# A decoder layer with a routed MoE: the overflow block moved directly behind the expert's gate-up

## The chip, the cores and the metric

The kernel runs on one core of a Trainium2 chip. The metric is the device time of one launch in microseconds, lower is better. All data is float32; TensorE (PE) multiplies, VectorE (DVE) and ScalarE (ACT) work on its results, GpSimd (POOL) does almost nothing here, and SyncE (SP) issues the DMAs that bring the weights from HBM.

## The reference

One layer of a decoder for 256 tokens of width 1024: a mixer of three kinds of attention, a layer norm, then a mixture of experts, and a second layer norm. Only the mixture of experts matters here. Each token goes to 4 of 32 experts, and each expert has 8 MB of gate-up weights (1024 x 2048) and 4 MB of down weights (1024 x 1024):

```python
logits = (xt @ router_w + router_b).astype(F32)
top_logit, top_e = lax.top_k(logits, TOP_K)            # 4 of 32
top_w = jax.nn.softmax(top_logit, axis=-1)
...
def expert_block(args):                                # for each expert's tokens
    e, tok, w = args
    xb = xt[tok]
    gu = xb @ w_gu[e] + b_gu[e]
    gate = jnp.minimum(gu[:, :D_EXPERT], SWIGLU_LIMIT)
    up = jnp.clip(gu[:, D_EXPERT:], -SWIGLU_LIMIT, SWIGLU_LIMIT)
    act = gate * jax.nn.sigmoid(SWIGLU_ALPHA * gate) * (up + 1.0)
    y = act @ w_dn[e] + b_dn[e]
    return (y * w[:, None]).astype(h.dtype)
...
out = jnp.zeros((T, D), h.dtype).at[buf_tok].add(ys.reshape(P, D))
```

All 402.7 MB of expert weights are read once.

## The kernel before

Every engine has its own program, written out by hand, and they are tied together by semaphores. After attention and routing (the first 200 us) the experts run in order 0 to 31, in a loop over 15 pairs (L1255 on PE) with the first and the last expert written out around it.

**Slots and overflow.** An expert has 64 slots (SLOTS). If more than 64 tokens chose it, the rest go in *extra blocks* of 32 slots (XSLOTS). How many extra blocks an expert has is known only at run time: a small table `nx` holds the counts, every engine reads its expert's entry into a register (`value_load`) and jumps over the extra block if it is zero.

**One expert on PE.** `gate_up` (L1109) multiplies the gathered tokens by the gate-up weights in four chunks of 2 MB, waiting for the DMA of each, and adds the bias with four short matmuls; each chunk counts up `guc`. DVE and ACT turn the result into activations (`activations`, L1687: minimum L1690, clip L1691, L1693, the sigmoid L714 on ACT, product L1696). Meanwhile PE fills the time: in an odd expert with `gather` (L1065), which gathers the tokens of the next pair of experts in two halves, copied out by ACT (L678); in an even expert with `combine` (L1073), which adds the outputs of a finished pair to the result in PSUM. Then `act_transposes` (L1144, its transposes are L1148) turns the activations, ACT copies them (L718), and `down` (L1133) multiplies by the down weights in four chunks of 1 MB, each counting up `dn_used`.

**One extra block on PE** (`extra_blocks`, L1214): it waits until two PSUM banks are free; gathers 32 tokens (`extra_gather`); ACT copies them (L691), two transposes (L1191), ACT copies again (L693); 36 gate-up matmuls, where each chunk counts up `xguc`; then it waits for activations of its own (DVE, ACT), transposes them (L1200, L1203), multiplies by the down weights (each chunk counts up `xdnc`), waits for ACT's copy of the result (L710) and adds it with `extra_combine`. DVE has its extra block behind the main activations, and prepares it ahead in `first_extra_slots` (L1740).

**The weights on SP.** There are two slots for gate-up weights, one for even and one for odd experts, and one slot for down weights. `next_gu` (L407) issues the gate-up weights of expert e+2 chunk by chunk (L354), as soon as expert e is through with that chunk; `next_dn` (L415) issues the down weights of e+1 (L359) as expert e is through with its own. SP runs them in one fixed order, gu of e+2, then dn of e+1, so that what stands behind waits for what stands in front (the last three pairs have the two the other way round). An expert with extra blocks is through with a chunk only when the block is, too:

```python
sp.wait_ge(s["guc"], i * (2 * GU_CHUNKS) + (par * GU_CHUNKS + c + 1))
sp.wait_ge(s["xguc"], xc)
load_gu(i + 1, par, c)
```

Line numbers of matmuls are those of the helper that issues them (L791 `mm`; transposes have the line of their call).

Of the kernel before, what the change touches and what calls it, by code (L numbers as in the profile page):

```python
# [57 lines left out]
def hybrid_layer(nc, x, w_in, b_in, pos_k, pos_v, w1_k, w2_k, w1_v, w2_v, g_out, w_out, ln1_g, ln1_b,  # L58
                 router_w, router_b, w_gu, b_gu, w_dn, b_dn, ln2_g, ln2_b, out):
    with ExitStack() as ctx:  # L60
# [480 lines left out]
        def _(act):  # L541
# [134 lines left out]
            def slots_to_sbuf(h, bank, n):  # L676
                act.wait_ge(s["ga"], n)
                act.activation(xg[:, 4 * h:4 * h + 4, :].rearrange("p k s -> p (k s)"), PB[bank][:, :], ACT.Copy)\  # L678
                   .then_inc(s["xg_ok"], 1)
# [6 lines left out]
            def extra_slots():  # L686

                act.reg_add(xcount, xcount, 1)
                xc = act.snap(xcount, min_val=1, max_val=96)
                act.wait_ge(s["xga"], xc)  # L690
                act.activation(xrows, PB[4][:, 0:256], ACT.Copy).then_inc(s["xgs"], 1)  # L691
                act.wait_ge(s["xgt"], xc)
                act.activation(yx[:, 0:KT * XSLOTS], PB[4][:, 256:512], ACT.Copy).then_inc(s["xxg"], 1)  # L693

            def extra_sigmoid():
                act.wait_ge(s["xgok"], act.snap(xcount, min_val=1, max_val=96))
                act.activation(act_x[0:64, :], gt[0:64, :], ACT.Sigmoid, scale=SWIGLU_ALPHA).then_inc(s["xsig"], 1)

            def extra_act_copy():
                xc = act.snap(xcount, min_val=1, max_val=96)  # L700
                act.wait_ge(s["xct"], xc)
                act.activation(CTx[:, :, :].rearrange("p b t -> p (b t)"), PB[7][:, 0:256], ACT.Copy)\
                   .then_inc(s["xctd"], 1)
                act.wait_ge(s["xat"], xc)
                act.activation(actTx[:, :, :].rearrange("p c s -> p (c s)"), PB[6][:, 0:256], ACT.Copy)\
                   .then_inc(s["xactT"], 1)

            def extra_outputs():
                act.wait_ge(s["xdnc"], act.snap(act.snap(xcount, min_val=0, max_val=96) * 4 + DN_CHUNKS, min_val=1, max_val=4 * 97))
                act.activation(yx, PB[6][:, :], ACT.Copy).then_inc(s["xyd"], 1)  # L710

            def sigmoid(n):
                act.wait_ge(s["g_ok"], n)
                act.activation(act_sb, gt, ACT.Sigmoid, scale=SWIGLU_ALPHA).then_inc(s["sig"], 1)  # L714

            def act_columns(bank, n):
                act.wait_ge(s["at"], n)
                act.activation(actT[:, :, :].rearrange("p c s -> p (c s)"), PB[bank][:, :], ACT.Copy)\  # L718
                   .then_inc(s["actT"], 1)

            def combine_weights(n):

                act.wait_ge(s["ct"], n)
                act.wait_ge(s["comb"], n)
                act.activation(CT[:, :, :].rearrange("p b t -> p (b t)"), PB[6][:, 0:256], ACT.Copy)\
                   .then_inc(s["ct_sb"], 1)

            def expert_output(e, n):
                act.wait_ge(s["dn_used"], n * DN_CHUNKS)
                act.activation(ysb[64 * e:64 * e + 64, 1, :], PB[7][64:128, :], ACT.Copy).then_inc(s["ysb_ok"], 1)  # L730

            def extra_blocks(t):
                n = act.value_load(nx[0:1, t:t + 1] if isinstance(t, int) else nx[0:1, bass.ds(t, 1)], min_val=0,
                                   max_val=MAX_EXTRA)
                with act.If(n > 0):
                    with act.Fori(0, n):
                        extra_slots()
                        extra_sigmoid()
                        extra_act_copy()
                        extra_outputs()  # L740
                act.nop()
# [10 lines left out]
            expert_output(0, 1)  # L752
            with act.Fori(0, PAIRS - 1) as i:
                sigmoid(2 * i + 2)
                slots_to_sbuf(0, 6, 2 * i + 3)
                act_columns(5, 2 * i + 2)
                slots_to_sbuf(1, 4, 2 * i + 4)
                extra_blocks(2 * i + 1)
                expert_output(1, 2 * i + 2)
                sigmoid(2 * i + 3)  # L760
                act_columns(5, 2 * i + 3)
                combine_weights(i + 2)
                extra_blocks(2 * i + 2)
                expert_output(0, 2 * i + 3)

            for b in range(TB):
# [16 lines left out]
        def _(pe):  # L783
# [6 lines left out]
            def mm(o, l, r, start, stop):  # L790
                return mm_(o, l, r, start=start, stop=stop, skip_group_check=True)  # L791
# [273 lines left out]
            def gather(h, bank, parts=range(4)):  # L1065
                for k in parts:
                    for b in range(TB):
                        ins = mm(PB[bank][:, P * k:P * k + P], x_sb[:, b, P * (4 * h + k):P * (4 * h + k) + P],
                                 oh[:, b, :], k == 0 and b == 0, b == TB - 1)
                if k == 3:  # L1070
                    ins.then_inc(s["ga"], 1)
# [8 lines left out]
            def gate_up_chunk(c, e):  # L1080

                for k in range(2 * c, 2 * c + 2):
                    for n in range(4):
                        ins = mm(PB[4 + n // 2][64 * (n % 2):64 * (n % 2) + 64, :], xg[:, k, 64 * e:64 * e + 64],
                                 gu_slot[e][:, k, 512 * n:512 * n + 512], k == 0, False)
                return ins
# [22 lines left out]
            def gate_up(e, loaded, n):  # L1109

                for c in range(GU_CHUNKS):
                    pe.wait_ge(s_gul[e][c], 16 * loaded)
                    gate_up_chunk(c, e).then_inc(s["guc"], 1)
                pe.wait_ge(s["oht"], n)
                gate_up_bias(e).then_inc(s["gu"], 1)
# [98 lines left out]
            def extra_blocks(e, loaded, t, pb4_pb6_copied, copies, outputs_copied):  # L1214

                count = pe.value_load(nx[0:1, t:t + 1] if isinstance(t, int) else nx[0:1, bass.ds(t, 1)], min_val=0,
                                      max_val=MAX_EXTRA)
                with pe.If(count > 0):
                    with pe.Fori(0, count):
                        pe.wait_ge(s[pb4_pb6_copied], copies)  # L1220
                        extra_gather()
                        for c in range(GU_CHUNKS):
                            extra_gate_up_chunk(c, e).then_inc(s["xguc"], 1)
                        extra_gate_up_bias(e).then_inc(s["xgu"], 1)

                        pe.wait_ge(s["ysb_ok"], outputs_copied + 1)
                        if not (isinstance(outputs_copied, int) and outputs_copied == 0):
                            pe.wait_ge(s["ysb_dv"], outputs_copied)
                        extra_act_transposes()
                        xc = pe.snap(xcount, min_val=1, max_val=96)  # L1230
                        pe.wait_ge(s["xctd"], xc)
                        pe.wait_ge(s["xactT"], xc)
                        for c in range(DN_CHUNKS):
                            pe.wait_ge(s_dnl[e][c], 16 * loaded)
                            extra_down_chunk(c).then_inc(s["xdnc"], 1)
                        extra_combine()
                pe.nop()
# [17 lines left out]
            with pe.Fori(0, PAIRS - 1) as i:  # L1255

                gate_up(1, i + 1, 2 * i + 2)
                pe.wait_ge(s["ohs"], i + 2)
                pe.wait_ge(s["ct_sb"], i + 1)
                gather(0, 6)  # L1260
                pe.wait_ge(s["g_ok"], 2 * i + 2)
                gather(1, 4, range(2))
                act_transposes(2 * i + 2)
                gather(1, 4, range(2, 4))
                extra_blocks(1, i + 1, 2 * i + 1, "xg_ok", 2 * i + 4, 2 * i + 1)
                down(1, i + 1, 2 * i + 2)

                pe.wait_ge(s["xg_ok"], 2 * i + 4)
                gate_up(0, i + 2, 2 * i + 3)
                pe.wait_ge(s["ysb_ok"], 2 * i + 3)  # L1270
                pe.wait_ge(s["ysb_dv"], 2 * i + 2)
                combine(range(3))
                act_transposes(2 * i + 3)
                weight_transposes()
                combine(range(3, 4))
                extra_blocks(0, i + 2, 2 * i + 2, "ct_sb", i + 2, 2 * i + 2)
                down(0, i + 2, 2 * i + 3)

            def outputs_of_30(b):
# [569 lines left out]
```

## Time and profile before

| what | value |
|---|---|
| median of 3 runs | 1151.54 us (1148.82 to 1151.68) |
| the profiled execution's own time | 1150.07 us |
| its span, on which all rows below stand | 1147.9 us |
| PE busy | 1073.4 us (94%) |
| DVE, ACT, POOL busy | 265.1, 152.4, 28.3 us |
| DMA moved | 426.32 MB, mean 371 GB/s |
| chain that ended last | PE 62%, DMA 30%, DVE 5% |

Times are microseconds from the start of the span. The time of the execution has 2.2 us around the span. "Busy" of PE counts pipelined matmuls with modelled ends, so 94% is not PE at its peak. The granted clock (PEclk) of 1.00 is 2.4 GHz, 0.50 is 1.2 GHz.

### The profile page before, as it was taken

To read this page: it belongs to the slowest core of one execution; us is meant where nothing else is said; L and a number is where in the kernel's file an instruction comes from. 1 tells how busy PE (TensorE), PEld (TensorE's weight loads), DVE (VectorE), ACT (ScalarE), POOL (GpSimd) and SP (SyncE) were. 2 spreads that over 40 slices of the span, in tenths; PEclk is the share of its full clock that TensorE was granted. 3 is DMA by queue.
4 is the path that set the end of the run, shared out by engine and by line. 5 is a ranking of instruction groups with operands and counts; after the bars stand their busy time and mean duration, and the time that the engine had idled before them with its cause. 6 is when DMAs were issued, how large, how long until landed. Compare 5 with 4: busy or idle time off the path is not lost.

```text
span 1147.9 us, 14752 instructions
## 1 busy us (share of the span) xinstructions
PE 1073.4 (94%) x5382; PEld 463.7 (40%) x5383; DVE 265.1 (23%) x770; ACT 152.4 (13%) x318; POOL 28.3 (2%) x54
## 2 busy tenths in 40 slices
PE   7999897998999999999999979999999999999995
PEld 6777644332343443323333333434343324343332
DVE  2354636111112111111111211121111111111124
ACT  2044511110010110100000010101010101010120
POOL 3000410000000000000000000000000000000000
PEclk9999998999999999999999989999999999999998
DMA  9723439939999999999999999999999999999993
GB/s 309 263 110 74 148 132 395 400 149 399 423 426 425 427 427 426 427 427 425 427 427 425 429 417 399 427 427 426 427 427 426 427 421 426 427 425 427 427 425 157
DMA packets 49268, 426.32 MB, mean 371 GB/s; under 512 B 5065, under 2 KB 8954, under 8 KB 16442
## 3 DMA queue, kind: packets, MB, share of 16 engines
q1 hardware_dynamic: 48666, 425.37, 89.7%
q10 hardware_dynamic: 576, 0.61, 0.2%
q8 instruction: 16, 0.26, 0.1%
q14 instruction: 10, 0.08, 0.0%
HBM read 424.91 MB, written 1.05 MB: 371 GB/s over the span
## 4 chain that ended last, share of the span: by engine, by line
PE 62%; DMA 30%; DVE 5%; issue 1%; SPq 1%; ACT 1%; DVEq 0%
PE PB L791 59%; DMA WB<-in_w_down_dram 26%; DMA WB<-in_w_gate_up_dram 3%; PE PB L1148 1%; DMA WB<-in_w_in_dram 1%; DVE S L1693 1%; DVE S L1696 1%; DVE S L1690 1%; DVE S L1691 1%; DVE S L1555 0%; DVE S L1815 0%; SPq L337 0%; DVE WB L1474 0%; DVE S L1589 0%; DVE K L1806 0%
## 5 line engine op out<-in xcount | busy, mean ns | idle before, releaser
L791 PE MATMUL PB<-WB,S 128*64 128x512 f32 (+5 forms) x3456 | 753.2, 590 | 31.1 <-DMA WB<-in_w_down_dram 24.2
L791 PEld LDWEIGHTS PB<-WB,S 128*64 128x64 f32 (+2 forms) x3456 | 253.5, 139 | 509.5 <-issue 441.7
L1690 DVE TENSOR_SCALAR S<-PB 128x512 f32<-128x512 f32 (+1 forms) x34 | 23.5, 691 | 482.1 <-PE PB L791 482.1
L791 PE MATMUL PB<-S 32*64 32x512 f32 (+5 forms) x464 | 108.7, 586 | 4.7 <-issue 2.4
L1734 DVE COPY S<-PB 64x512 f32<-64x512 f32 x31 | 21.2, 683 | 264.6 <-PE PB L791 264.6
L714 ACT ACTIVATE S<-S 128x512 f32<-128x512 f32 x32 | 20.2, 632 | 456.2 <-DVE S L1690 456.1
L791 PEld LDWEIGHTS PB<-S,X 128*128 128x128 f32 x512 | 62.7, 200 | 13.3 <-issue 12.2
L791 PE MATMUL PB<-S,X 128*128 128x128 f32 x512 | 66.8, 286 | 1.0 <-DVE S L1633 1.0
L791 PE MATMUL PB<-S,WB 128*128 128x256 f32 (+2 forms) x336 | 60.2, 377 | 1.0 <-DMA WB<-in_w_in_dram 0.6
L791 PEld LDWEIGHTS PB<-S 32*64 32x64 f32 (+5 forms) x464 | 33.0, 147 | 67.6 <-issue 62.1
L791 PE MATMUL PB<-WB 128*32 128x128 f32 (+9 forms) x284 | 48.1, 362 | 5.3 <-DVE WB L1520 2.8
L791 PEld LDWEIGHTS PB<-S,WB 128*128 128x128 f32 (+1 forms) x336 | 46.5, 170 | 12.4 <-issue 2.1
L730 ACT ACTIVATE S<-PB 64x512 f32<-64x512 f32 x31 | 18.4, 595 | 240.7 <-PE PB L791 240.7
L791 PEld LDWEIGHTS PB<-WB 128*64 128x64 f32 (+3 forms) x284 | 30.3, 153 | 18.7 <-issue 12.6
L530 POOL TENSOR_TENSOR K<-K 128x1 f32<-128x1 f32 x4 | 3.1, 766 | 968.3 <-DVE K L1809 956.5
L718 ACT ACTIVATE S<-PB 128x512 f32<-128x512 f32 x32 | 19.1, 598 | 56.7 <-PE PB L1148 56.7
L1148 PEld LDWEIGHTS PB<-K,S 128*128 128x128 f32 x128 | 18.1, 210 | 17.2 <-DVE S L1696 16.4
L1148 PE MATMUL PB<-K,S 128*128 128x128 f32 x128 | 23.7, 308 | 1.4
L1696 DVE TENSOR_TENSOR S<-S 128x512 f32<-128x512 f32 (+1 forms) x34 | 23.5, 691 | 1.8 <-ACT S L714 0.7
L1693 DVE SCALAR_TENSOR_TENSOR S<-S 128x512 f32<-128x512 f32 (+1 forms) x34 | 23.5, 692 | 1.2
L1691 DVE TENSOR_SCALAR S<-PB 128x512 f32<-128x512 f32 (+1 forms) x34 | 23.2, 682 | 0.1
L678 ACT ACTIVATE S<-PB 128x512 f32<-128x512 f32 x32 | 19.1, 598 | 20.8 <-PE PB L791 20.8
(219 smaller groups left out, 353.1 us busy)
## 6 DMA issues: line engine op xcount, KB each, us to landing
WB<-in_w_gate_up_dram SPq DMA_DIRECT2D x128, 2048.0 KB, 24.8
WB<-in_w_down_dram SPq DMA_DIRECT2D x128, 1024.0 KB, 21.1
WB<-in_w_in_dram SPq DMA_DIRECT2D x3, 2048.0 KB, 16.0
WB<-in_w_in_dram SPq DMA_DIRECT2D x1, 2144.0 KB, 11.0
WB<-in_w_in_dram SPq DMA_DIRECT2D x2, 1024.0 KB, 10.8
WB<-in_w_out_dram SPq DMA_DIRECT2D x2, 1024.0 KB, 10.0
WB<-in_w_out_dram SPq DMA_DIRECT2D x1, 2048.0 KB, 7.9
WB<-in_w_in_dram SPq DMA_DIRECT2D x1, 1040.0 KB, 12.7
```

The source lines that it names most:

```text
L530: pool.tensor_tensor(st[:, o + 2:o + 3], st[:, o + 1:o + 2], half[:, 0:1], ALU.pow).then_inc(s["lnp"], 1)
L678: act.activation(xg[:, 4 * h:4 * h + 4, :].rearrange("p k s -> p (k s)"), PB[bank][:, :], ACT.Copy)\
L714: act.activation(act_sb, gt, ACT.Sigmoid, scale=SWIGLU_ALPHA).then_inc(s["sig"], 1)
L718: act.activation(actT[:, :, :].rearrange("p c s -> p (c s)"), PB[bank][:, :], ACT.Copy)\
L730: act.activation(ysb[64 * e:64 * e + 64, 1, :], PB[7][64:128, :], ACT.Copy).then_inc(s["ysb_ok"], 1)
L791: return mm_(o, l, r, start=start, stop=stop, skip_group_check=True)
L1148: ins = tr(PB[5][:, P * c:P * c + P], every_fourth(act_sb, c), ident)
L1690: ts(g, gate, LIMIT, None, ALU.min).then_inc(s[g_ok], 1)
L1691: ts(u, up, LIMIT, -LIMIT, ALU.min, ALU.max).then_inc(s[clip], 1)
L1693: stt(u, u, 1.0, g, ALU.add, ALU.mult).then_inc(s[upg], 1)
L1696: tt(a, u, a, ALU.mult).then_inc(s[done], 1)
L1734: cp(ysb[64 * e:64 * e + 64, 0, :], PB[7][0:64, :]).then_inc(s["ysb_dv"], 1)
```

## The change

In the loop over pairs the extra block moves. In the odd expert of a pair it stood behind `gather` and `act_transposes`, directly ahead of `down`; now it stands directly behind `gate_up`, ahead of `gather`. In the even expert it stood behind `combine` and the transposes; now it stands ahead of `combine`. What it waits for at its start is now `g_ok`, DVE's minimum, which frees the PSUM bank PB4 (it was ACT's copy of the gathered tokens in the odd, and of the combine weights in the even expert). ACT's program is put in the same order: its extra block follows the sigmoid. DVE, SP, the blocks of experts 0 and 31, and the work itself stay as they are.

```diff
@@ ACT, loop over pairs
                 sigmoid(2 * i + 2)
+                extra_blocks(2 * i + 1)
                 slots_to_sbuf(0, 6, 2 * i + 3)
                 act_columns(5, 2 * i + 2)
                 slots_to_sbuf(1, 4, 2 * i + 4)
-                extra_blocks(2 * i + 1)
                 expert_output(1, 2 * i + 2)
                 sigmoid(2 * i + 3)
+                extra_blocks(2 * i + 2)
                 act_columns(5, 2 * i + 3)
                 combine_weights(i + 2)
-                extra_blocks(2 * i + 2)
                 expert_output(0, 2 * i + 3)
@@ PE, loop over pairs
                 gate_up(1, i + 1, 2 * i + 2)
                 pe.wait_ge(s["ohs"], i + 2)
                 pe.wait_ge(s["ct_sb"], i + 1)
+                extra_blocks(1, i + 1, 2 * i + 1, "g_ok", 2 * i + 2, 2 * i + 1)
                 gather(0, 6)
                 pe.wait_ge(s["g_ok"], 2 * i + 2)
                 gather(1, 4, range(2))
                 act_transposes(2 * i + 2)
                 gather(1, 4, range(2, 4))
-                extra_blocks(1, i + 1, 2 * i + 1, "xg_ok", 2 * i + 4, 2 * i + 1)
                 down(1, i + 1, 2 * i + 2)
 
                 pe.wait_ge(s["xg_ok"], 2 * i + 4)
                 gate_up(0, i + 2, 2 * i + 3)
+                extra_blocks(0, i + 2, 2 * i + 2, "g_ok", 2 * i + 3, 2 * i + 2)
                 pe.wait_ge(s["ysb_ok"], 2 * i + 3)
                 pe.wait_ge(s["ysb_dv"], 2 * i + 2)
                 combine(range(3))
                 act_transposes(2 * i + 3)
                 weight_transposes()
                 combine(range(3, 4))
-                extra_blocks(0, i + 2, 2 * i + 2, "ct_sb", i + 2, 2 * i + 2)
                 down(0, i + 2, 2 * i + 3)
```

## Rows read from the trace of the kernel before

**Rows 1.** The page: what the DMA engines moved in 40 equal slices.

```profile
GB/s 309 263 110 74 148 132 395 400 149 399 423 426 425 427 427 426 427 427 425 427 427 425 429 417 399 427 427 426 427 427 426 427 421 426 427 425 427 427 425 157
```

**Rows 2.** The chain that ended last, in order of time: start, length, what.

```profile
296.63 25.50 PE PB L791 x130
...
349.37 25.50 PE PB L791 x130
...
467.00 27.29 DMA WB<-in_w_down_dram
...
496.53 27.27 DMA WB<-in_w_down_dram
...
1086.81 4.72 PE PB L791 x24
```

**Rows 3.** Timeline, the lines with LDWEIGHTS show the wait: PE at the extra block of expert 1.

```profile
241.45 1.09 PE L791 MATMUL PB<-S 32*64 32x512 f32 x8
...
242.61 0.69 DVE L1690 TENSOR_SCALAR S<-PB 128x512 f32<-128x512 f32 x1 [10.97 <-PE PB L791]
...
245.99 1.06 PE L791 MATMUL PB<-S,X 128*128 128x128 f32 x8
...
247.08 0.60 ACT L678 ACTIVATE S<-PB 128x512 f32<-128x512 f32 x1 [0.30 <-PE PB L791]
...
247.86 1.07 PE L791 MATMUL PB<-X,S 128*32 128x256 f32 x16 [0.82 <-ACT S L678]
...
250.34 7.07 PE L791 MATMUL PB<-WB,S 128*32 128x512 f32 x64 [0.47 <-ACT S L693]
...
263.05 5.28 PE L791 MATMUL PB<-WB,S 128*32 128x512 f32 x32 [0.52 <-issue]
...
270.96 20.82 PE L791 MATMUL PB<-WB,S 128*64 128x512 f32 x96
```

**Rows 4.** Timeline of SP: the issues behind the extra block of expert 1.

```profile
252.49 5.47 SPq L354 DMA_DIRECT2D WB<-in_w_gate_up_dram  x4
273.16 5.48 SPq L359 DMA_DIRECT2D WB<-in_w_down_dram  x4
```

**Rows 5.** The same behind the extra block of expert 15.

```profile
668.53 5.46 SPq L354 DMA_DIRECT2D WB<-in_w_gate_up_dram  x4
689.55 5.48 SPq L359 DMA_DIRECT2D WB<-in_w_down_dram  x4
```

**Rows 6.** Stretches: length, busy of PE, PEld, DVE, ACT, POOL; PEclk, DMA share, GB/s.

```profile
245.00:249.00 4.00, 3.12 (x32) 2.11 (x30) 0.67 (x3) 1.36 (x4) 0.00 (x0) 1.00 0.00 0
...
261.00:265.00 4.00, 3.00 (x18) 1.43 (x22) 0.42 (x1) 0.77 (x2) 0.00 (x0) 0.75 1.00 430
...
273.00:277.00 4.00, 4.00 (x20) 1.29 (x18) 0.00 (x0) 0.00 (x0) 0.00 (x0) 1.00 0.85 276
...
670.00:672.00 2.00, 2.00 (x25) 0.52 (x17) 0.00 (x0) 0.00 (x0) 0.00 (x0) 1.00 0.85 344
```

**Rows 7.** Timeline: PE behind the gate-up of expert 30.

```profile
1090.39 3.86 PE L791 MATMUL PB<-S 32*64 32x512 f32 x14
...
1094.34 0.75 PE L1148 MATMUL PB<-K,S 128*128 128x128 f32 x4
...
1096.10 10.52 PE L791 MATMUL PB<-WB,S 128*64 128x512 f32 x48
```

**Rows 8.** Timeline: PE around its first jump over an extra block (expert 0).

```profile
211.02 1.18 PEld L791 LDWEIGHTS PB<-S 128*128 128x128 bf16 x10
...
212.43 0.19 PEld L791 LDWEIGHTS PB<-S 128*128 128x128 f32 x1 [0.24 <-issue]
...
217.58 0.70 PE L791 MATMUL PB<-S 128*128 128x512 f32 x1 [2.41 <-issue]
```

**Rows 9.** Who waited for whom: total us, times, longest.

```profile
DVE K L1764 <- issue: 17.2, 16, 1.4
```

**Rows 10.** DMA queues, only 300 to 640 us: packets, MB, share.

```profile
q8 instruction: 1, 0.02, 0.0%
```

## The prediction

> **What bounds the kernel now.** I read the page's slices first. From the tenth slice to the last but one the DMA engines move 425 to 427 GB/s almost without a gap [rows 1]: the expert weights alone are 402.7 MB, 943 us at 427 GB/s. So the experts are bound by the stream of weights, and what can be won is the time in which the stream stands still. PE's 94% busy must not mislead; the chain shows who is late. An expert costs PE 26.4 us where the chain runs on PE alone (52.74 us from one x130 group to the next, which is a pair) and 29.5 us where it runs over the landing of down weights [rows 2]. PE has 3.1 us to spare for each expert and catches up after each delay. The stream is hurt only where SP has nothing to issue.
>
> Next, where the overflow blocks are. The narrow matmuls (128*32) occur in two places in the whole trace, at expert 1 (248 to 271 us) and, with the same pattern, at expert 15 (664 to 687 us). Both are odd. The other 28 experts in the loop jump over the block. Around expert 1 the stream stands completely still until gate-up weights are issued at 252.49 us, and after them it has a second, smaller hole: 276 instead of 427 GB/s around 273 us [rows 4, 6]. Around expert 15 there is hardly a first hole (344 GB/s for 2 us at 670 us) and then one at 690 us, with the down weights issued at 689.55 us [rows 5, 6].
>
> **What the change does to the two blocks.** The block moves ahead of the 16 gathering matmuls (of 128 columns) and the four transposes. Before: the bias of gate-up ends at 241.45 + 1.09 = 242.54 us, and the block's own gather begins at 247.86, 5.32 us later [rows 3]. Of these, 4.51 us are work (to 245.99 + 1.06 = 247.05), 0.81 is the wait for ACT's copy. After: the block waits for DVE's minimum, which ends at 242.61 + 0.69 = 243.30 us. Before, the block began 0.18 us behind the copy (247.08 + 0.60 = 247.68); with the same step it will begin at 243.48. It starts **4.4 us earlier**, and so does `xguc`: SP issues gate-up weights for expert 3 at about 248.1 us instead of 252.49, and those for expert 17 at about 664.1 instead of 668.53 [rows 4, 5].
>
> **Why this brings next to nothing.** SP has a fixed order: behind four chunks of gate-up weights come four of down weights, and these wait for `down` of the same expert. The four gate-up chunks are 8.39 MB, 19.6 us at 427 GB/s. Issued at 252.49 they keep the engines busy to about 273 us, and the down weights are issued at 273.16: the two just meet. Issued at 248.1 they are through at about 269, and **the stream stands still for the same 4.4 us behind them**, since `down` is still last on PE. Its start was the gate-up's end + 4.51 (gather, transposes) + 0.81 (wait) + 23.10 (the block, 247.86 to 270.96) = 28.42 us. It becomes 0.94 (wait for DVE) + 23.10 + 4.51 = 28.55. Sum: +0.13 us for a block. A few terms come off or on: the transposes waited 0.1 us or so for the main activations, which are now long done. ACT reads its count behind the sigmoid now (DVE's reading and jumps show 17.2 us in 16 cases, 1.1 each, 1.4 at most [rows 9]); that runs in the shadow of PE's gather in the block, and costs up to 0.7 us where it doesn't. I take +0.1 for a block, between -0.8 (the wait vanishes) and +0.8. For expert 15 the working is the same; the small hole at 670 us closes (344 of 427 GB/s for 2 us is 0.4 us) and opens again ahead of 690.
>
> What is queued behind the new waits: on PE everything, but it is the same work in another order, and none of the delayed pieces has a user before `down`: ACT's copies of the gathered tokens lie under `down`, 16 matmuls of two passes each, 32 of the 96 that take 20.82 us, so 6.9 us [rows 3]. The block now asks for expert 15's down weights 4.4 us earlier, near 675 instead of 679 us; the hole at 670 shows that SP's queue had run dry, so all that was issued before had arrived [rows 6]. On SP nothing is moved. DVE's order stays; its activations of the block still wait for the block's gate-up, 14 us behind the minimum.
>
> Do both additions reach the end? Yes: with the down weights' issue the stream starts again and doesn't stop, so 0.1 us there is 0.1 us at the end, twice: **+0.2 us**.
>
> **TensorE's clock** is the largest uncertain term. In both blocks PE waits some 3 us for the block's activations, and the granted clock is 0.75 in the mean of 261 to 265 us [rows 6], a mix of 2.4 and 1.2 GHz. The block's 32 rows of down matmuls take 5.28 us; its 64 rows of gate-up take 7.07, so 32 would take 3.54 at full clock [rows 3]. The low clock costs 1.74 us a block. The wait stays, so I leave the term as it is; but the stretch of low clock may come to lie wholly in the wait (-1.74), or reach further, over the gather that now follows (+1.74). Two blocks: -3.5 to +3.5 us, both ends unlikely.
>
> **What it does to the experts without a block.** PE reads the count and jumps directly behind the gate-up. For 27 of the 28 the price is under the 3.1 us that PE has to spare [rows 2]. Not so for expert 30, behind which nothing is left to catch up: its last gate-up chunk lands at 1086.8 us and from there the chain is PE's [rows 2]. There, bias and three combine matmuls end at 1090.39 + 3.86 = 1094.25, and the transposes, which wait for the activations, begin at 1094.34 [rows 7]. The cover is 0.09 us; whatever stands between bias and combine beyond that is on the path. How long does PE stand at a read and a jump? Before, at expert 0: eight short bf16 matmuls, the read, the jump, then combine, whose weight loads follow with the usual idle of 0.24 us and not more [rows 8]. So at most 0.24, and I take 0, since PE's front has 4.7 us of matmuls (last chunk and bias) in hand to run ahead, against 1.4 at most for DVE's read. In the old place, ahead of `down`, it was free as well: the 1.76 us from 1094.34 to 1096.10 are filled by six transposes (four take 0.75) and a combine matmul ((3.86 - 1.09) / 3 = 0.92) [rows 3, 7]. So nothing comes back.
>
> **Forecast: no difference that can be measured.** 1150.07 + 0.2 = 1150.3 us for the profiled execution. Against the median of the runs, 1.5 us above it, 1151.54 + 0.2 = **1151.7 us**.
>
> **Rivals.**
> First, **faster, since the stream starts earlier**. The gate-up slot is given back 4.4 us sooner; if the time behind it were not taken back by the down weights, the kernel would win 4.4 us at expert 1 and the 0.4 us of the hole at expert 15: 4.8 us, 1146.7 us. For it: the still stand before 252.49 us is the longest in the experts (0 GB/s from 245 to 249 us [rows 6]). Against it: down weights are issued at 273.16, exactly where the gate-up weights end, and 276 GB/s there shows that the engines have nothing else [rows 4, 6]. Its weaker form is a clock that falls better, up to -3.5. Chance 5% for over 0.3%.
>
> Second, **slower, by the jump behind the gate-up**. Place: expert 30, and the start of both blocks. Behind the very first jump over an extra block PE stood for 2.41 us with nothing to wait for ("issue") in the midst of a combine [rows 8]. If a jump in its new place brings such a stop each time, it costs 2.41 - 0.09 = 2.3 us at expert 30, and at the two blocks what a read (1.4 us) takes beyond the wait of 0.81, 0.6 each: 3.5 us, 1155.1 us. It decides from 0.09 us on at expert 30; at the others PE's 3.1 us cover it. Against it: from 300 to 640 us, some twelve experts with as many jumps, the queue of instruction fetches has a single packet [rows 10], so the loop's code isn't fetched anew, and I take the 2.41 us for those of a first passage. The Trainium skill (Runtime: NRT & Kernel Launch, Instruction fetch mechanics) has a rule that speaks for this rival: a taken branch out of the fetched window stalls the engine until the page is there. The trace doesn't bear it out for a repeated loop. Chance 7%, with a clock that falls worse 9% for all over 0.3%.
>
> Third, **the change reaches more experts than two**: that in even experts the block no longer waits for `combine_weights`. It can't, since no even expert has a block; the time is that of the forecast, and it is in its chance.
>
> **How the numbers follow.** Forecast 86%, first rival 5%, second with the clock 9%. A measurement of this kernel tells 0.3%, 3.45 us, from no change. The range takes in the terms of the sum (-0.8 to +0.8 a block, most of the clock's swing, up to 2.3 at expert 30), and leaves the first rival's full size out: 1148.3 to 1155.1 us.
>
> **What would show it.** In the profile of the changed kernel: the narrow gather begins 0.8 to 1.0 us behind the bias, at 243.5 us (step 1); SP's gate-up issue behind expert 1 is at 248.1 (step 2); the down weights' issue stays at 273.2 to 273.4 and 689.6 to 689.9, and the stream has a hole of over 4 us ahead of it (step 3); the transposes of expert 30 still begin 0.1 us behind the third combine (step 4). I am wrong if the down weights' issue comes over 1 us sooner or later, which would be the clock or PE's front, or if the stream has no hole there.

## The result: 2 us slower, within what counts as no change

| | before | changed |
|---|---|---|
| median (20 runs each) | 1150.47 us | 1152.49 us |
| lowest, highest | 1148.82, 1152.61 | 1149.42, 1154.98 |
| ratio, 95% interval | | 1.0017 (1.0009 to 1.0024) |
| profiled execution, its span | 1150.07, 1147.9 us | 1152.66, 1150.5 us |

The forecast was 1151.7 us and no measurable difference. The ratio is 2.0 us of loss (1.0 to 2.8), clear of zero and below 3.45 us. The forecast's +0.2 us is too small; where the rest comes from is what the experiments are about. That 1151.7 lies only 0.8 us from 1152.49 is in part luck: it was built on a median of three runs, 1151.54, which is 1.1 us above the median of twenty, and this offsets more than half of the 1.8 us that the forecast lacks.

First the page of the changed kernel, what the DMA engines moved in 40 slices. It answers to [rows 1]:

```profile
GB/s 311 269 101 74 158 131 394 406 196 334 425 427 424 427 426 427 427 426 427 426 427 426 427 416 369 426 427 426 427 425 426 427 423 426 427 426 427 426 426 159
```

The stream has the same two dips. In the first the ninth slice has 196 GB/s instead of 149, the tenth 334 instead of 399: the gate-up weights come earlier, and the standstill has moved behind them.

The timeline of PE and its neighbours in the changed kernel, at the block of expert 1, answers to [rows 3]:

```profile
240.72 1.09 PE L791 MATMUL PB<-S 32*64 32x512 f32 x8
241.87 0.69 DVE L1690 TENSOR_SCALAR S<-PB 128x512 f32<-128x512 f32 x1 [10.97 <-PE PB L791]
242.75 1.07 PE L791 MATMUL PB<-X,S 128*32 128x256 f32 x16 [0.94 <-DVE S L1690]
...
244.31 0.44 PE L1191 MATMUL PB<-K,S 128*128 128x128 f32 x2 [0.50 <-ACT S L691]
...
245.23 8.77 PE L791 MATMUL PB<-WB,S 128*32 128x512 f32 x64 [0.47 <-ACT S L693]
...
259.63 5.03 PE L791 MATMUL PB<-WB,S 128*32 128x512 f32 x32 [0.52 <-issue]
...
267.30 2.94 PE L791 MATMUL PB<-S,X 128*128 128x128 f32 x24
...
270.08 0.64 PE L1148 MATMUL PB<-K,S 128*128 128x128 f32 x4
...
271.54 20.82 PE L791 MATMUL PB<-WB,S 128*64 128x512 f32 x96
```

Everything before it ran 0.73 us earlier than in the profile of before, so stretches are to be compared, not points in time. The order is the new one: the narrow gather begins 0.94 us behind the bias (240.72 + 1.09 = 241.81), the wide gather stands behind the block. One length is not as before: the 64 rows of the block's gate-up take 8.77 us instead of 7.07.

SP's issues in the changed kernel, behind expert 1 and behind expert 15, answer to [rows 4, 5]:

```profile
248.93 5.60 SPq L354 DMA_DIRECT2D WB<-in_w_gate_up_dram  x4
273.74 5.48 SPq L359 DMA_DIRECT2D WB<-in_w_down_dram  x4
...
666.07 5.47 SPq L354 DMA_DIRECT2D WB<-in_w_gate_up_dram  x4
692.18 5.48 SPq L359 DMA_DIRECT2D WB<-in_w_down_dram  x4
```

And stretches of 2 us of the changed kernel (columns as in [rows 6]), first in the block's gate-up, then ahead of the issue of the down weights at 273.74:

```profile
244.00:246.00 2.00, 1.21 (x10) 0.43 (x14) 0.93 (x3) 0.64 (x2) 0.00 (x0) 0.86 0.00 0
246.00:248.00 2.00, 2.00 (x16) 0.58 (x12) 0.00 (x0) 0.00 (x0) 0.00 (x0) 0.50 0.00 0
248.00:250.00 2.00, 2.00 (x20) 0.52 (x16) 0.00 (x0) 0.00 (x0) 0.00 (x0) 0.79 0.26 49
...
268.00:270.00 2.00, 2.00 (x21) 2.00 (x20) 0.00 (x0) 0.60 (x1) 0.00 (x0) 1.00 0.93 393
270.00:272.00 2.00, 2.00 (x17) 1.62 (x17) 0.00 (x0) 0.95 (x2) 0.00 (x0) 1.00 0.04 8
272.00:274.00 2.00, 2.00 (x12) 0.72 (x10) 0.00 (x0) 0.25 (x1) 0.00 (x0) 1.00 0.00 0
```

The kernel before, in the last 2 us ahead of its issue of the down weights at 273.16:

```profile
271.00:273.00 2.00, 2.00 (x12) 0.73 (x12) 0.00 (x0) 0.00 (x0) 0.00 (x0) 1.00 1.01 434
```

Two things are seen. The granted clock is 0.50, that is 1.2 GHz, from 246 to 248 us, in the middle of dense matmuls; that is the longer gate-up. And the stream stands still for some 4 us ahead of the down weights (8 and 0 GB/s), where the kernel before has full speed, 434 GB/s, up to 273 us.

Where the 2.6 us between the two profiled spans lie:

| stretch | before | changed | difference |
|---|---|---|---|
| start to the bias of expert 1 | 241.45 | 240.72 | -0.73 |
| bias to the issue of down weights, expert 1 | 31.71 | 33.02 | +1.31 |
| from there to the bias of expert 15 | 384.35 | 384.31 | -0.04 |
| bias to the issue of down weights, expert 15 | 32.04 | 34.13 | +2.09 |
| from there to the end | 458.35 | 458.32 | -0.03 |

The first row lies ahead of all that was changed; it is what one execution differs from another. Of the rest every difference lies between gate-up and down weights of the two experts with a block. The 28 others, and the tail behind expert 30, give nothing.

### The profile page after: what moved, and what is told of

It is laid out like the page before. It is cut to its first block, busy times and chain, and to the rows that moved or that the text cites. A ratio compares the mean times of both kernels' runs of the same rounds, so it can differ in the third digit from the quotient of the medians.

```text
span 1150.5 us, 14750 instructions
## 1 busy us (share of the span) xinstructions
PE 1076.6 (94%) x5382; PEld 464.2 (40%) x5383; DVE 264.9 (23%) x770; ACT 151.9 (13%) x318; POOL 28.3 (2%) x54
## 4 chain that ended last, share of the span: by engine, by line
PE 62%; DMA 30%; DVE 5%; issue 1%; SPq 1%; ACT 1%; DVEq 0%
PE PB L791 59%; DMA WB<-in_w_down_dram 26%; DMA WB<-in_w_gate_up_dram 3%; PE PB L1148 1%; DMA WB<-in_w_in_dram 1%; DVE S L1690 1%; DVE S L1693 1%; DVE S L1696 1%; DVE S L1691 1%; DVE S L1555 0%; DVE S L1815 0%; SPq L337 0%; DVE WB L1474 0%; DVE S L1589 0%; DVE K L1806 0%
```

## The experiments

The theory: nothing is lost in the order as such; **the clock** is. In the new order a stretch of 1.2 GHz falls into the block's gate-up, where it hadn't been in the profile of before. Rivals: the luck of one profile (it falls where it will, in either order, and the 2 us come from elsewhere), and the jumps directly behind the gate-up. In the following, "path" is the stretch from the bias to the issue of down weights, first for expert 1, then for expert 15; "gate-up" and "down" are the times that the block's 64 gate-up and 32 down matmuls of the trace take, its rows.

### Both kernels again, and the two halves of the change

The changed kernel once more:

> The changed kernel, unaltered, a second profile and more times. Clock theory (the order brings a stretch of 1.2 GHz into the block's gate-up, since the pauses now lie directly behind the expert's gate-up): the 64 rows of the block's gate-up take 8.3 to 8.8 us in both blocks again, not the 7.07 of before, and the ratio is 1.001 to 1.0025. Rival, luck of one profile (the low stretch may fall anywhere in either order): at least one of the two takes 7.07 us here. Rival, the jumps in even experts: gate-up may take anything, the tail behind expert 30 is longer than before by 1 us or more.

Measured: 1.0012 (1.0003 to 1.0020). Gate-up 8.64 and 7.07 us, path 32.79 and 31.93. The transposes of expert 30 begin 0.09 us behind the third combine, as before. The ratio is as the theory said, but its "both blocks" is wrong, and the luck rival's condition is met by the second block.

The odd experts' half alone, as diff against before:

```diff
@@ PE
                 pe.wait_ge(s["ct_sb"], i + 1)
+                extra_blocks(1, i + 1, 2 * i + 1, "g_ok", 2 * i + 2, 2 * i + 1)
                 gather(0, 6)
...
                 gather(1, 4, range(2, 4))
-                extra_blocks(1, i + 1, 2 * i + 1, "xg_ok", 2 * i + 4, 2 * i + 1)
@@ ACT
                 sigmoid(2 * i + 2)
+                extra_blocks(2 * i + 1)
                 slots_to_sbuf(0, 6, 2 * i + 3)
                 act_columns(5, 2 * i + 2)
                 slots_to_sbuf(1, 4, 2 * i + 4)
-                extra_blocks(2 * i + 1)
```

> Only the odd experts' block is moved, the even experts' stays behind combine. Clock theory: both blocks that run are odd, so the whole loss is here, +1.9 us, ratio 1.001 to 1.0025, block gate-ups of 8.3 to 8.8 us. Jump rival: most of the loss is gone, ratio under 1.0007.

Measured: 1.0033 (1.0020 to 1.0046), gate-up 8.56 and 7.07, down 6.53 and 6.00, path 34.36 and 32.59. The whole loss is here, and more than was expected; five runs don't say whether it really is more than the full change's, whose interval it overlaps.

The even experts' half alone is the rest of the change's diff:

> Only the even experts' block is moved; none of them has one, so what is moved is the reading of the count and the jump, behind the gate-up. Clock theory: nothing, ratio 0.9993 to 1.0007, and the transposes of expert 30 begin 2.8 us behind the start of the minimum as before. Jump rival: +1.5 us or more, ratio 1.0013 or above, and a gap on TensorE between bias and combine.

Measured: 1.0005 (0.9995 to 1.0014), path 31.71 and 31.58. PE's timeline in the even half alone, behind the gate-up of expert 30:

```profile
1091.22 3.86 PE L791 MATMUL PB<-S 32*64 32x512 f32 x14
1095.17 0.74 PE L1148 MATMUL PB<-K,S 128*128 128x128 f32 x4
```

1091.22 + 3.86 = 1095.08, and 0.09 us later the transposes: the same as [rows 7], with the reading of the count and the jump now in between. The jump rival is out at expert 30, the place where nothing would have covered it. The interval alone would leave room for 1.6 us in all, but the odd half has the whole loss and none of these jumps in the even experts.

The kernel before once more:

> The kernel before, unaltered, for a second profile. Clock theory: the block's gate-up takes 7.07 us in both blocks, the block's down 5.3 us. Luck rival: one of the gate-ups takes over 8 us here.

```profile
247.88 8.77 PE L791 MATMUL PB<-WB,S 128*32 128x512 f32 x64 [0.47 <-ACT S L693]
...
665.75 7.07 PE L791 MATMUL PB<-WB,S 128*32 128x512 f32 x64 [0.47 <-ACT S L693]
```

That is the timeline of PE in this second profile of before. The theory's expectation is wrong: the low stretch falls into the gate-up in the old order, too, here at expert 1. So it can't be "the new order has it, the old one not". What is left is a matter of how often. This execution also shows one source of the swing from run to run (3.8 us over 20 runs of the kernel before, 5.6 of the changed one) that has nothing to do with the change: the bias of expert 1 comes at 238.99 instead of 241.45 us. From 216 to 224 us, behind the jump over expert 0's block, the granted clock is 1.00 in the mean here and 0.79 in the first profile, and the way from there to the bias of expert 1 is 1.3 us shorter.

### Filling the pauses

If the clock falls for the pauses ahead of the block's gate-up, matmuls in these pauses must keep it up. The fillers multiply the identity by a tile into PSUM bank PB7, and nobody reads the result. The block's two waits for the copies out of PB7 move to its start (this part of the edit is not shown):

```diff
+            def filler(columns, n=1):
+                for _ in range(n):
+                    mm(PB[7][:, 0:columns], ident, x_sb[:, 0, 0:columns], True, True)
 ...
+                        filler(512)
                         pe.wait_ge(s[pb4_pb6_copied], copies)
 ...
+                filler(256)
                 pe.wait_ge(s["xgs"], xc)
 ...
+                filler(256)
                 pe.wait_ge(s["xxg"], xc)
```

> The changed kernel with idle matmuls (identity by a tile, into a free PSUM bank, not used) in the three short pauses at the start of a block: 0.86 us in the wait for the minimum, 0.43 us in each of the two waits for ACT's copies. Clock theory (the low stretch in the block's gate-up follows from the pauses before it): both gate-ups take 7.07 us, ratio against before near 1.000 (0.999 to 1.001), some 1.9 us under the changed kernel. Chance rival (the low stretch falls where it will, whatever PE does before): one gate-up in two still takes over 8 us, ratio 1.001 to 1.002.

Measured: 1.0041 (1.0027 to 1.0054). Gate-up 7.07 and 7.07, as the clock theory said, and path 32.25 and 32.18 against the 33.02 and 34.13 of the changed kernel. But the time is worse, by 4.7 us against before, where at most some 1 us had been expected. The stretches say where: the bias of expert 1 comes at 243.34 us, later than in any profile so far (238.99 to 242.09). The loss is ahead of the first block.

> The changed kernel with three idle matmuls (2.6 us) in the block's wait for its activations alone. Clock theory: the block's down rows take 3.5 us instead of 4.9 to 6.4, in both blocks, 1.5 to 3 us less each; the gate-up keeps its lottery; ratio against before 0.998 to 0.9995. Chance rival: the down rows stay at 5 us or more, ratio 1.001 to 1.002.

Here three fillers of 512 columns stand in the wait for the block's activations, behind the bias of its gate-up. Measured: 1.0027 (1.0017 to 1.0037), slower than expected. Down rows 3.64 and 3.64 us, with a granted clock of 1.00 all through them; gate-up 8.53 and 8.77; path 31.49 and 31.73. And again a late start: bias at 244.82 us. PE's timeline of this kernel around its first jump, which answers to [rows 8]:

```profile
211.32 1.04 PE L791 MATMUL PB<-S 128*128 128x256 bf16 x8
217.01 3.57 PE L791 MATMUL PB<-S 128*128 128x512 f32 x4 [4.65 <-issue]
```

The stop behind the jump over expert 0's block is 4.65 us and comes ahead of the combine's float32 passes. In [rows 8] it was 2.41 us and stood ahead of the combine's last pass, and it is 1.5 to 2.4 us in all eleven profiles whose expert 0 has the block as it was. The stop does not end later, though: PE goes on 6.8 to 7.7 us behind the start of expert 0's bias in all fourteen profiles, the three with fillers there (6.9 to 7.3) among them. What differs is how much PE had done before it stood.

> The same three idle matmuls in the order of before. Clock theory: down rows at 3.5 us, 1.7 us less for each block, ratio 0.996 to 0.998 (-2.5 to -4.5 us). Chance rival: no change, 0.9995 to 1.0005.

The same in the old order. Measured: 0.9994 (0.9985 to 1.0003), down rows 3.64 and 3.64, gate-up 7.07 and 8.77, path 30.06 and 31.75, the stop 4.92 us. The mechanism is there, the gain is not: three fillers in a pause win some 1.6 us a block, and their code in expert 0's block costs 3 to 4 us once: from the bias of expert 0 to that of expert 1 it is 34.2 to 34.8 us in the three kernels with fillers there, and 29.5 to 31.6 in the eleven others.

So the fillers were put into the loop's odd block alone:

> The changed kernel with idle matmuls in the three pauses at the start of a block, as in fill_start, but only in the loop's odd block, so that the code of expert 0's block keeps its length. Clock theory: both gate-ups of the blocks take 7.07 us; from the bias of gate-up to the issue of down weights 32.2 us as in fill_start (32.25 and 32.18). Code-length theory of fill_start's loss (added code in expert 0's block lengthens the one stop behind the first jump from 1.9 to 4.6 us): the stop is 1.8 to 2.4 us here, ratio against before 1.000 to 1.0015, under fill_start by 2 to 4 us. Rival (the idle matmuls themselves cost): ratio 1.003 or more.

Measured: 1.0004 (0.9995 to 1.0013). Gate-up 7.07 and 7.07, path 32.43 and 32.35, the stop 1.52 us. By the ratios that is +0.5 us, 4.2 us less than fill_start, so the fillers themselves are not what cost there, and 1.5 us less than the changed kernel, whose interval this one overlaps. Its timeline and stretches at expert 1, to be read beside those of the changed kernel above:

```profile
243.24 1.12 PE L791 MATMUL PB<-X,K 128*128 128x512 f32 x2
244.30 1.07 PE L791 MATMUL PB<-X,S 128*32 128x256 f32 x16
245.30 0.70 PE L791 MATMUL PB<-X,K 128*128 128x256 f32 x2
245.87 0.44 PE L1197 MATMUL PB<-K,S 128*128 128x128 f32 x2
246.15 0.60 PE L791 MATMUL PB<-X,K 128*128 128x256 f32 x2
...
246.00:248.00 2.00, 1.96 (x16) 0.76 (x20) 0.44 (x3) 0.38 (x1) 0.00 (x0) 1.00 0.00 0
248.00:250.00 2.00, 2.00 (x24) 0.65 (x20) 0.00 (x0) 0.00 (x0) 0.00 (x0) 1.00 0.33 66
```

The three lines with "PB<-X,K" are the fillers; PE has no pause, and the clock stays at 1.00.

All profiles together, the gate-ups of the blocks that took 8.3 to 8.8 us instead of 7.07:

| order at the block (early pauses filled or not) | profiles | gate-ups with low clock |
|---|---|---|
| as before, pauses not filled | 6 | 2 of 12 |
| as changed, pauses not filled | 5 | 7 of 10 |
| as changed, pauses filled | 3 | 0 of 6 |

(The experiments on delays and fill_wait_before count in the first row, fill_wait and work_in_wait in the second, work_and_fill in the third; those on delays and on real work follow below.) If the order made no difference, 7 of 10 against 2 of 12 or more extreme would come in 1.7% of cases, and 7 of 10 against 0 of 6 in 1.0% (in this direction alone). The difference sits at expert 1 (5 of 5 against 1 of 6); at expert 15 it is 2 of 5 against 1 of 6, which shows nothing by itself. It is not proof of each block, but it is how the sum comes out: a low stretch costs 1.3 to 1.7 us, and half a one more for each block makes +1.6 us for the two. That is near the 2.0 measured.

The runs that were not profiled have a record, too: the mean granted clock of each. It is 0.982 or less in 14 of 32 runs of the changed kernel and in 2 of 68 runs of the kernel before, 0.9823 and 0.9841 in the mean. As an estimate, 0.0018 of 1150 us is some 2 us, which is what the difference costs if PE is busy all through it. And in the twenty runs of the table above, the ten with 0.982 or less took 1153.4 us in the mean, the ten others 1151.1. The record doesn't say where in a run the clock was low: fill_start_odd has 0.9826 in the mean of its 11 runs, as low as the changed kernel, and loses hardly anything. Its stretches at the blocks' wait and down rows have 0.74 in the mean over 13 us (254 to 267 and 671 to 684), the first profile of before has 0.87 and 0.74, the second 0.87 and 0.87; while PE waits, a low clock costs nothing.

### Does a microsecond at the block reach the end, and one elsewhere not?

Three fillers (2.6 us) ahead of `down`, in the order of before, once in the odd blocks (the first lines) and once in the 13 odd experts that have none (the last):

```diff
                         extra_combine()
+                        if delayed:
+                            filler(512, 3)
 ...
+                with pe.If(count < 1):
 ...
+                    filler(512, 3)
 ...
                 down(1, i + 1, 2 * i + 2)
```

The second also reads the count once more ahead of this, and waits for the copies out of PB7 ahead of the fillers.

> The order of before with three idle matmuls (2.6 us) at the end of each odd block, ahead of down. Theory (the issue of down weights behind a block restarts the stream, so each us there is a us at the end): two blocks, +5.1 us, ratio 1.0035 to 1.0055; clock may shift it by 1 us. Rival (the stream's start, set by the gate-up slots, is what counts): ratio 0.9995 to 1.001.

Measured: 1.0051 (1.0038 to 1.0064), +5.9 us, path 35.38 and 35.60 instead of some 31.9. What is lost between gate-up and down weights at a block is lost at the end.

> The order of before with the same 2.6 us of idle matmuls ahead of down in the 13 odd experts of the loop that have no block, 33 us in all. Theory (PE has 3.1 us to spare for each expert): +0 to +0.5 us, ratio 0.9995 to 1.001. Rival (PE is the bound): up to +33 us, ratio 1.01 to 1.03.

Measured: 1.0081 (1.0068 to 1.0094), +9.1 us of the 33 added. Neither answer. Its path and the 384 us between the blocks are untouched (31.65, 384.04, 32.16); all of it lies behind expert 15, 467.26 us instead of 458.35. The chain of waits of this kernel says why:

```profile
712.11 25.50 PE PB L791 x130
...
768.02 25.50 PE PB L791 x130
...
823.92 25.50 PE PB L791 x130
...
1047.48 25.50 PE PB L791 x130
```

55.9 us for each pair, and the chain is on PE and the activations to the end; before it was 52.7 us [rows 2], and the chain was back on the DMA by 853 us. As an estimate from these: PE recovers 6.3 us with each pair (59.0 - 52.7), and it took some three pairs, so after a block PE is some 20 us behind. With the delays it recovers only 3.1 us a pair and never gets the chain back to the DMA before the experts end. From 900 to 950 us the stream itself falls to 392 GB/s, where it had 426. PE's spare time is free only once it has caught up.

### Real work instead of idle matmuls

The wait of 3.1 us for the block's activations can take work that has to be done anyway: the main transposes and the half of the gather that goes to bank PB4. `extra_body` is the block of `extra_blocks` with these two behind its gate-up's bias; ACT's copies are put in the same order. The half of an odd expert with and without a block:

```diff
+                with pe.If(count > 0):
+                    pe.wait_ge(s["g_ok"], 2 * i + 2)
+                    extra_body(1, i + 1, 2 * i + 1, transposes_and_half)
 ...
+                gather(0, 6)
+                with pe.If(count < 1):
+                    pe.wait_ge(s["g_ok"], 2 * i + 2)
+                    gather(1, 4, range(2))
+                    act_transposes(2 * i + 2)
+                    gather(1, 4, range(2, 4))
```

> An odd expert with a block does real work in the block's wait for its activations: the main transposes and the second half of the gather (2.8 us), which thereby leave the path; without a block the order is that of the change. Theory (down weights' issue sets the stream, and every us that the path from gate-up to down loses is won): 2.8 us less for each block and a clock that stays up for the down rows (1.5 to 2): down weights of expert 2 issued at about 269 us instead of 273, ratio 0.992 to 0.996 against before. Rival (the stream is bound elsewhere): ratio 0.999 to 1.001.

Measured: 0.9977 (0.9961 to 0.9993), -2.6 us, less than expected. Gate-up 8.70 and 7.07, down 3.64 and 3.64, path 29.29 and 27.66. At expert 15 the path lost what it should, 4.4 us against before; at expert 1 it lost 2.4, since the gate-up had its low stretch, and the down weights were issued at 271.62 us, not at 269. And the end gained less than the paths. The rest of the kernel behind the second path took 460.61 us instead of 458.35: down weights were issued at 683.99, but the stream was running at 377 GB/s or more in every 2 us from 660 to 694 us. Here it has no hole left to close, and for this part the rival was right. The runs of this kernel spread from 1144.2 to 1152.1 us, four of twelve above 1150, for which no profile shows the reason.

> work_in_wait, with the idle matmuls of fill_start_odd in the three early pauses of the odd block. Clock theory: gate-up and down rows of both blocks at full clock (7.07 and 3.64 us), 27.9 us from bias to down weights in both; ratio against before 0.996 to 0.998, 0.5 to 1.5 us under work_in_wait. Chance rival: one gate-up of two over 8 us, ratio as work_in_wait's.

The same with the fillers of fill_start_odd. Measured: **0.9952 (0.9936 to 0.9968), -5.5 us, clearly faster than before and after, and the lowest median of all kernels** (its interval just overlaps that of work_in_wait). Gate-up 7.07 and 7.07, down 3.64 and 3.64, path 27.72 at expert 15. At expert 1 this profile has a path of 34.42, where 27.9 was expected, and its timeline shows the place:

```profile
260.53 1.99 PE L815 MATMUL PB<-S 64*128 64x512 f32 x8 [0.71 <-ACT S L710]
266.64 3.78 PE L815 MATMUL PB<-S,X 128*128 128x128 f32 x16 [4.13 <-issue]
```

A stop of 4.13 us with nothing to wait for, at the first passage behind the taken block. Two of its six runs are at 1148.3 to 1148.4 us, the profiled one among them, the other four at 1143.2 to 1145.6; whether the other slow one had the same stop is not known. The queue of instruction fetches has two packets from 255 to 268 us there. But the profiles of before and of work_in_wait have one in the same stretch and no such stop, so that code was fetched late here is likely and not shown.

## Why the prediction was right, and which step was too small

The mechanism of the weights' stream was as forecast, and the loss stayed within what counts as no change. The prediction named a sign of being wrong: down weights issued over 1 us later, "which would be the clock or PE's front". That sign came, at both blocks (path +1.31 and +2.09 us), and it was the clock.

**What bounds the kernel: right**, with one correction. The stream, its two holes and the places of the blocks are as read. But "PE's 3.1 us cover it" holds only where PE has caught up; delay_elsewhere lost 9.1 us behind expert 15 by it. The forecast didn't need it, since no trace shows a cost of the jump in its new place.

**Step 1, the start of the block: right.** 0.94 us behind the bias, as worked out.

**Step 2, the earlier gate-up issue: right at full clock.** From the end of the bias to SP's issue it was 9.95 us; with a gate-up at full clock it is 665.56 - 660.00 = 5.56 (after_again, expert 15), 4.4 us less. With the low stretch at its start it is 7.12.

**Step 3, the stream stands still behind it instead: right.** The hole of some 4 us ahead of 273.74 is in the rows above, and delay_in_block shows that the issue of down weights is what counts. Rival one, the earlier stream, had nothing: no kernel was faster by an earlier gate-up alone.

**The path without the clock: right within 0.1 us.** Taking the excess of gate-up over 7.07 and of down over 3.64 from each path, five of the six paths of before, before_again and even_only come to 30.06 or 30.07 us and one to 30.36; those of the two profiles of the changed kernel come to 29.9 to 30.2. The forecast was +0.1.

**The clock term: mis-sized, and this is the failed step.** The prediction gave it both ends, -1.74 and +1.74 a block, and took the middle, 0, with the argument that the wait stays. It looked only at the stretch of low clock that the profile of before showed, in the down rows. The one that costs is another, at the block's gate-up, which the profile of before happened not to have. Its price is 1.3 to 1.7 us, and it comes in 7 of 10 gate-ups instead of 2 of 12: the term should have been some +0.8 us a block. The down rows went on varying: 5.0 to 6.3 us in the old order, 5.4 in the mean of the ten whose wait was not filled, and 4.9 to 6.5 us in the new one, 5.7 in the mean of six; a term of +0.3 there is not clear of that spread. The ends given were nearly kept: path +1.31 and +2.09. A small error beside it: the full-clock time of the 32 down rows is 3.64 us, as fill_wait shows, not 3.54, so the low clock cost 1.64 us there and not 1.74.

**The second rival, the jump: wrong for this change, right as a mechanism.** Behind expert 30 nothing (0.09 us in both, and in even_only). But unexplained stops do exist at first passages, and code added to expert 0's block lengthened one from about 2 us to 4.6 to 4.9.

What is still open: why the low stretch comes more often at the block's gate-up in the new order; why filling the early pauses leaves the down rows at 5.5 to 5.8 us, longer than before's 5.3 (all four have a clock of 0.74 in the mean of the 13 us around them, where the two profiles of before have it once in four); and whether the odd half alone is really slower than the whole change.

## What to carry to other kernels

Look where a freed buffer's next user stands in its queue: a load that starts 4 us earlier wins nothing if the next one in order waits for work that has not moved. Where PE's path sets the restart of a stream, count the pauses on it, and put work that has to be done anyway into the longest; it pays twice, by itself and by the clock. A term that one profile shows at one place is a draw from several: take a second execution of the unchanged kernel before you call it fixed, and compare stretches between fixed marks, so that what was lost elsewhere isn't charged to the change.

## What the runs showed of the hardware

**The clock falls without one long pause.** In the changed kernel PE was busy for 1.51 us (1.07 + 0.44) of the 3.42 us between bias and block gate-up, with three pauses of 0.94, 0.50 and 0.47 us, and the granted clock was 0.86 in the mean of 244 to 246 us and 0.50 from 246 to 248, in dense matmuls that had already begun. With the pauses filled it stayed at 1.00 there, in six of six cases. The same pauses in the old order (0.82, 0.50, 0.47 us) lie behind 4.5 us of small matmuls, and the clock fell in 2 of 12 cases. The same kernel met it in one execution and not in another (7.07 and 8.77 us at expert 1 of before). The Trainium skill (TensorE: Matmul & The Clock Gate, Part 1) says as much of the start of a kernel: the number of matmuls at low clock varies from run to run. The traces agree, and show it in the middle of a kernel.

**Code costs at its first passage.** Behind 200 us, all stops of PE over 1 us with no reason in the profile, of 1.5 to 4.9 us, were at a place that PE reached for the first time, behind a jump or a block that had been run through; later passages of the loop had none. The Trainium skill (Runtime: NRT & Kernel Launch, Instruction fetch mechanics) has the rule that a taken branch out of the fetched window stalls the engine. The traces fit it where the code hasn't been run yet, and show no such stop at later passages; that the stops are fetches is argued from this, not shown. The stop at expert 0 ended at the same distance behind expert 0's bias in all fourteen profiles (6.8 to 7.7 us), whatever was jumped over. It began earlier with three matmuls more in the block: 4.6 to 4.9 us, with seven or eight of the combine's eight passes still to do, instead of 1.5 to 2.4 us ahead of the last one. Whether the length of the block does this, or only where the code behind it comes to lie, was not tested.
